# Chunk gating: two norms folded into column factors and one number per token, LayerNorm's affine in the mixing's eviction, mixing between the u units

## The chip, the cores and the metric

The kernel is one program on one core of a Trainium2 chip (trn2). The metric is device time of one execution in microseconds, as a median of runs. A profiled execution gives the trace; its own time stands beside its span below.

## The reference

Two transformer-like blocks work on 512 tokens of 1024 channels in float32. The change lies where the first block ends and the second begins.

```python
h = h + conv_ffn(hn, ...)                      # end of the first block ("ffout" in the kernel)
x = rms_norm(h, norm_final_g)                  # output of the first block, the second block's residual stream
y = _rms_norm(x, mix_norm_g[0])
# _chunk_gating_mixer(y, ...)
uv = gelu(y @ w_in, approximate=False)         # w_in: 1024 x 2048
u, v = split(uv, 2)
v = layer_norm(v, ln_g, ln_b)                  # over 1024 channels of a token
v = v.reshape(B, 4, 128, 8, 128)               # 4 chunks of 128 tokens, 8 groups of 128 channels
w = where(causal, w_s, 0)                      # 8 x 128 x 128
gate = einsum('gts,bnsgc->bntgc', w, v) + b_s  # mixes positions in a chunk
x = x + (u * gate) @ w_out
```

`rms_norm(x, g)` is `x * rsqrt(mean(x * x) + eps) * g` with the mean over a token's channels. 

## The kernel before

Channels lie on the 128 partitions in eight tiles (`h[:, m, :]` is 128 channels by 512 tokens), tokens on the free axis. Each fp32 product is made of three matmuls with operands split into a high part in fp32r and the rest (`mm3`, L425 to L429): high by high, low by high, high by low. Weights come as a stream of units of 512 KB (128 x 1024): SyncE's queue loads a unit into one of two `raw` buffers (L450), ScalarE copies it to the high part (`hi`, L896), VectorE subtracts for the low part (`lo`, L1160), and there are four slots. `hi(u)` and `lo(u)` prepare unit u + 3, and `hi` waits until the unit four before it has been multiplied. A unit is 24 matmuls of 512 columns.

Each engine has its program written out by hand; all order is by semaphores. TensorE accumulates a unit in one of two PSUM banks (0 and 1), and VectorE evicts it (`s_free`). `residual` (L1179 ff.) adds an evicted unit to `h`; ScalarE then makes `xhi` (L904) and a square (L908), VectorE `xlo` (L1166), GpSimd adds up squares in `ssum` (L1682). `norm` (L516) multiplies `ssum` with a matrix of ones, ScalarE takes the root (L912), VectorE the reciprocal (L1171) into `rbc`, which the evictions of the next stage multiply with (`rows`, L1198).

After the last feed-forward residual ("ffout") the order is this. `norm("ffout")`; VectorE scales `h` tile by tile with `rbc` and the final gain (L1429), and ScalarE, VectorE and GpSimd make `xhi`, `xlo` and the squares of the scaled tiles ("final1"). cgv: the v half of the projection with tokens on the output's partitions, two halves f of four units, in each 96 matmuls; within the first, after two units, `norm("final1")`; after it `rbc` is transposed (L699) and one column per token block copied to `rtok`, by which the gelu's eviction scales (L1042). cgu: eight u units, evicted to `uf` (L1198), gelu in place (L1049). Beside them v is prepared: statistics (L1454, L1456), `layer_norm` on VectorE (L1466), gain and shift along the channels on GpSimd (L1725, L1726), and the split of v (L1175, L1176). Then mixing: eight groups of 12 matmuls of 128 columns each. VectorE adds the position bias, multiplies with u and splits (L1483 ff.), and cgout, eight units of the output projection, follows.

## Time and profile before

| | us |
|---|---|
| median of 3 runs | 1997.72 (1996.34 to 1999.89) |
| profiled execution | 1995.45 |
| its span | 1993.7 |
| TensorE busy | 1929.3 (97%) |
| VectorE busy | 1148.2 (58%) |
| ScalarE busy | 657.5 (33%) |
| GpSimd busy | 175.9 (9%) |
| granted TensorE clock, mean | 0.983 |

Busy time is the sum of instruction durations. A matmul's end is modelled and matmuls overlap: one of 512 columns is shown with 0.39 us, while the next starts 0.23 us later. So durations of TensorE are read from start to start or from a stretch, and a row of a busy share near 100% says nothing of speed. [...]

### The profile page before, as it was taken

The numbers are of one execution on the slowest core, as the hardware profiler recorded it, in microseconds if no ns is written. First come the engines' busy times: TensorE is split into PE (matmuls) and PEld (weight loads), VectorE is DVE, ScalarE is ACT, GpSimd is POOL, SyncE is SP. The second block draws the span as 40 slices with busy tenths as digits, with TensorE's granted clock in tenths as the row PEclk, the third lists the DMA queues.
The fourth block names the chain that finished last, engine by engine and source line by source line (L and its number), as shares of the span: only waits on it lengthen the run. The fifth ranks groups of instructions, "written<-read, shape, count | busy, mean of one in ns | idle before, by whom it ended". The sixth has DMA issues, their size and how long they took to land.

```text
span 1993.7 us, 24668 instructions
## 1 busy us (share of the span) xinstructions
PE 1929.3 (97%) x9086; PEld 1587.7 (80%) x9086; DVE 1148.2 (58%) x1454; ACT 657.5 (33%) x871; POOL 175.9 (9%) x167
## 2 busy tenths in 40 slices
PE   6989999999999999799999999999999999999998
PEld 4878888778888887588888888888788777888886
DVE  5774767757766523777553245346666776424532
ACT  5214545343333322432322122323333343212221
POOL 2000221220000000240100000100000020000000
PEclk9989999999999999897999999999999999999998
DMA  4212222223323333221233353222222213232331
GB/s 139 75 58 70 75 68 70 85 83 108 95 95 95 105 106 106 97 84 63 93 100 96 97 135 98 93 96 79 74 69 80 64 48 116 95 98 93 97 103 64
DMA packets 55565, 177.64 MB, mean 89 GB/s; under 512 B 5891, under 2 KB 12179, under 8 KB 55356
## 3 DMA queue, kind: packets, MB, share of 16 engines
q1 hardware_dynamic: 46800, 168.32, 26.7%
q10 hardware_dynamic: 8684, 8.18, 1.5%
q8 instruction: 59, 0.97, 0.2%
q14 instruction: 22, 0.18, 0.0%
HBM read 173.26 MB, written 2.13 MB: 88 GB/s over the span
## 4 chain that ended last, share of the span: by engine, by line
PE 87%; DVE 8%; ACT 2%; issue 1%; DMA 1%; POOL 1%; ACTq 0%; DVEq 0%; SPq 0%; POOLq 0%
PE ps L427 27%; PE ps L428 27%; PE ps L429 27%; DVE wlo L1160 1%; PE ps L622 1%; PE ps L751 1%; PE ps L435 1%; PE ps L780 1%; PE ps L763 1%; DVE rbc L1171 1%; POOL ssum L1682 1%; PE ps L781 0%; PE ps L516 0%; DMA lgb<-lngb 0%; DVE vr L1176 0%
## 5 line engine op out<-in xcount | busy, mean ns | idle before, releaser
L427 PE MATMUL ps<-xhi,whi 128*128 128x512 f32 x1592 | 635.9, 399 | 20.5 <-DVE wlo L1160 12.9
L429 PE MATMUL ps<-xlo,whi 128*128 128x512 f32 x1592 | 623.1, 391 | 0.0
L428 PE MATMUL ps<-xhi,wlo 128*128 128x512 f32 x1592 | 622.8, 391 | 0.0
L1160 DVE TENSOR_TENSOR wlo<-raw,whi 128x1024 fp32r<-128x1024 f32 x317 | 408.8, 1290 | 259.4 <-ACT whi L896 258.6
L896 ACT ACTIVATE whi<-raw 128x1024 fp32r<-128x1024 f32 x317 | 333.0, 1053 | 526.7 <-PE ps L429 448.8
L427 PEld LDWEIGHTS ps<-xhi,whi 128*128 128x128 f32 x1592 | 300.7, 189 | 93.3 <-issue 16.5
L429 PEld LDWEIGHTS ps<-xlo,whi 128*128 128x128 f32 x1592 | 300.4, 189 | 64.0
L428 PEld LDWEIGHTS ps<-xhi,wlo 128*128 128x128 f32 x1592 | 300.9, 189 | 60.3 <-issue 1.4
L427 PE MATMUL ps<-mh,whi 128*128 128x512 f32 x512 | 199.3, 389 | 0.0
L428 PE MATMUL ps<-mh,wlo 128*128 128x512 f32 x512 | 199.2, 389 | 0.0
L429 PE MATMUL ps<-mh,whi 128*128 128x512 f32 x512 | 199.2, 389 | 0.0
L1059 ACT ACTIVATE ms<-mr 128x512 f32<-128x512 f32 x64 | 40.4, 632 | 229.0 <-DVE mr L1498 229.0
L427 PEld LDWEIGHTS ps<-mh,whi 128*128 128x128 f32 x512 | 96.1, 188 | 20.3 <-issue 0.4
L429 PEld LDWEIGHTS ps<-mh,whi 128*128 128x128 f32 x512 | 96.1, 188 | 20.1
L428 PEld LDWEIGHTS ps<-mh,wlo 128*128 128x128 f32 x512 | 96.1, 188 | 19.9
L1682 POOL TENSOR_TENSOR ssum<-ssum,sq 128x512 f32<-128x512 f32 x55 | 80.7, 1467 | 287.1 <-ACT sq L908 285.1
L1191 DVE TENSOR_TENSOR h<-h,ps 128x512 f32 x48 | 33.0, 688 | 105.6 <-PE ps L429 105.6
L1498 DVE SCALAR_TENSOR_TENSOR mr<-ps,rbc 128x512 f32<-128x512 f32 x64 | 44.2, 690 | 80.0 <-PE ps L429 80.0
L1679 POOL COPY ssum<-sq 128x512 f32<-128x512 f32 x8 | 5.7, 706 | 911.2 <-ACT sq L908 911.2
L904 ACT ACTIVATE xhi<-h,par 128x512 fp32r<-128x512 f32 (+1 forms) x48 | 34.6, 722 | 143.8 <-DVE h L1191 126.3
L427 PE MATMUL ps<-hid,whi 128*128 128x512 f32 x176 | 68.5, 389 | 0.0
L428 PE MATMUL ps<-hid,wlo 128*128 128x512 f32 x176 | 68.5, 389 | 0.0
(290 smaller groups left out, 2154.3 us busy)
## 6 DMA issues: line engine op xcount, KB each, us to landing
raw<-wst SPq DMA_DIRECT2D x317, 512.0 KB, 3.5
h<-xT ACTq DMA_DIRECT2D x8, 256.0 KB, 6.4
out<-h SPq DMA_DIRECT2D x8, 256.0 KB, 2.1
oP<-oB ACTq DMA_DIRECT2D x16, 66.0 KB, 2.2
lgb<-lngb ACTq DMA_DIRECT2D x1, 1024.0 KB, 7.3
bias_a<-bias_rows ACTq DMA_DIRECT2D x4, 256.0 KB, 9.4
...
```

What stands on the lines that cost most here:

```text
L427: pe.matmul(o, w[0], x[0], start=first, stop=False, **kw)
L428: pe.matmul(o, w[1], x[0], start=False, stop=False, **kw)
L429: return pe.matmul(o, w[0], x[1], start=False, stop=done, **kw)
L435: ins = pe.matmul(o, w[a], v[b], start=first and i == 0, stop=i == 2, skip_group_check=True)
L622: ins = pe.matmul(o, w, sspr[:, part, x, CO[d]:CO[d] + T - P * d], start=False, stop=True, skip_group_check=True)
L896: act.activation(whi[:, n % SLOTS, :], raw[:, n % 2, :], ACT.Copy).then_inc(s_hi, 1)
L904: act.activation(xhi[:, m, :], hm, ACT.Copy, scale=par[:, 8 * g + m:8 * g + m + 1] if mi is None else par[:, bass.ds(mi + 8 * g, 1)]).then ...
L1059: act.activation(ms[:, m % 2, :], mr[:, m % 2, :], ACT.Square).then_inc(s_ms, 1)
L1160: dve.tensor_tensor(wlo[:, n % SLOTS, :], raw[:, n % 2, :], whi[:, n % SLOTS, :].bitcast(F32), ALU.subtract).then_inc(s_split, 1)
L1191: dve.tensor_tensor(hm, hm, bank((a + m) % 2), ALU.add).then_inc(s_free, 1)
L1498: dve.scalar_tensor_tensor(mr[:, m % 2, :], acc, 0.0, rbc[:, :], ALU.max, ALU.mult).then_inc(s_free, 1)
L1682: ins = pool.tensor_tensor(ssum[:, :], ssum[:, :], sq[:, n % 2, :], ALU.add)
```

## The change

The two norms in front of the gating become column factors and one number per token. With h the residual and g the final gain, `rms_norm(rms_norm(h, g), g2)` is h times g times g2 (per channel, made once as `G_X1`) times one number per token, 1 / sqrt(mean((g*g + eps) * h * h) + eps * eps). So "ffout" makes `xhi`/`xlo` directly from `h` with the factor `G_X1`, and two squares per tile: of `h`, and of `h` times sqrt(g*g + eps) (`G_C1`). GpSimd sums both (`ssum`, `ssum2`); TensorE reduces them to one number per token (`token_sums`), and `spread` writes both numbers out over a bank each. `h` itself is scaled with the final norm during the second half of cgv (`first_block_normed`).

LayerNorm's gain and shift leave v. Both are per channel, which is the partition of the mixing's output: the gain multiplies there in the eviction, and the shift times the sum of a row of the mixing weights is added to the position bias (`wsf` times ones on TensorE, then eight operations on `bsb`). ScalarE makes v's high part. GpSimd's two operations per token block and the 1 MB load of `lgb` go.

The mixing groups stand behind u units 3 to 7 (`SPATIAL_BEHIND`), and the u units accumulate in banks 6 and 7. The first two output units take their first six k tiles each before the last two (`early=6`).

The diff is cut to its core; left out are semaphore names, buffers, constants and the loading of the two LayerNorm rows as columns of `par`.

```diff
+CGU_BANKS = (6, 7)
+SPATIAL_BEHIND = {3: (0,), 4: (1, 2), 5: (3, 4), 6: (5, 6), 7: (7,)}
...
+            def two_units(u, a, xs, early):
+
+                for ks in (range(early), range(early, UT)):
+                    for j in range(2):
+                        if ks[0] == 0:
+                            unit_ready(u + j)
+                            acc_wait(a + j)
+                        for k in ks:
+                            ins = mm3(pe, bank((a + j) % 2), w_tile((u + j) % SLOTS, k), xs(k), k == 0, k == UT - 1)
+                        if ks[-1] == UT - 1:
...
+            def token_sums():
+
+                pe.wait_ge(s_ss, S0["ffout"] + 2 * KD)
+                for n, src in enumerate((ssum2, ssum)):
+                    for t in range(NT):
+                        ins = pe.matmul(bank(7)[:, NT * n + t:NT * n + t + 1], src[:, t * P:(t + 1) * P], ones[:, 0:1],
+                                        start=n == 0 and t == 0, stop=True, skip_group_check=True)
+                ins.then_inc(s_cts, 1)
+
+            def spread():
+
+                pe.wait_ge(s_ctk, 1)
+                for n in range(2):
+                    for t in range(NT):
+                        ins = pe.matmul(bank(7 - n)[:, t * P:(t + 1) * P], rtk[:, NT * n + t:NT * n + t + 1].to_broadcast([P, P]), ident,
+                                        start=t == 0, stop=True, skip_group_check=True)
+                ins.then_inc(s_csp, 1)
+
+            def positions_mixed(g):
+
+                if g == 0:
+                    pe.wait_ge(s_r, R0["ug"])
+                    pe.wait_ge(s_wsr, 1)
+                    pe.wait_ge(s_bs2, 1)
+                if g >= 4:
+                    pe.wait_ge(s_sgv, g - 3)
+                for t in range(NT):
+                    ins = mm3(pe, bank(2 + g % 4)[:, t * P:(t + 1) * P], (vr[:, 0, t, g * P:(g + 1) * P], vr[:, 1, t, g * P:(g + 1) * P]),
+                              (wsr[:, 0, g, :], wsr[:, 1, g, :]), t == 0, True, skip_group_check=True)
...
-                        norm("final1")
+                        token_sums()
                     if f == 0 and j == 3:
-                        pe.wait_ge(s_rb, N0["final1"] + 1)
...
-            dense(U0["cgu"], A0["cgu"], full(8), x_tile)
-            pe.wait_ge(s_r, R0["ug"])
-            pe.wait_ge(s_cdv, 2)
...
+            pe.wait_ge(s_cpo, 1)
+            pe.wait_ge(s_cac, 4)
+            for n in range(2):
+                ins = pe.matmul(bank(4 + n), ones, wsf[:, 4 * n:4 * n + 4, :], start=True, stop=True)
+            ins.then_inc(s_wsm, 1)
+            pe.wait_ge(s_h2, KD)
+            for m in range(KD):
+                dense(U0["cgu"] + m, A0["cgu"] + m, full(1), x_tile, banks=CGU_BANKS)
+                for g in SPATIAL_BEHIND.get(m, ()):
+                    positions_mixed(g)
...
+            act.wait_ge(s_gns, 1)
+            act.activation(par[:, 8 * G_C1:8 * G_C1 + KD], par[:, 8 * G_C1:8 * G_C1 + KD], ACT.Sqrt, bias=eps[:, 0:1]).then_inc(s_gnc, 1)
...
-            residual("ffout", 2, 12, 4, None, "ffout")
+            act.wait_ge(s_gnc, 1)
+            with act.Fori(0, 2, 1) as i:
+                for m in range(4):
+                    for j in range(3 * m, 3 * m + 3):
+                        hi(U0["ffout"] + j, i, 12)
+                    act.wait_ge(s_free, at(A0["ffout"] + m + 1, i, 4))
+                    sn, k = S0["ffout"] + 2 * m, i * 4 + m
+                    act.wait_ge(s_ss, at(sn, i, 8))
+                    gain = lambda g: par[:, bass.ds(k + 8 * g, 1)]
+                    act.activation(xhi[:, k, :], h[:, k, :], ACT.Copy, scale=gain(G_X1)).then_inc(s_xhi, 1)
+                    act.activation(sq[:, 0, :], h[:, k, :], ACT.Square).then_inc(s_sqd, 1)
+                    act.activation(sq[:, 1, :], h[:, k, :], ACT.Square, scale=gain(G_C1)).then_inc(s_sqd, 1)
...
-            act.dma_start(lgb[:, :, :], lngb.partition_broadcast(P)).then_inc(s_cld, 16)
-            for m in range(KD):
-                act.wait_ge(s_rb, N0["ffout"] + 1)
-                act.wait_ge(s_cv, KF + m + 1)
-                x_hi(m, None, G_MIX2, S0["final1"] + m)
...
+            hi(U0["cgv"] + 1)
+            act.wait_ge(s_cts, 1)
+            for n, e in enumerate((eps2, eps)):
+                act.activation(rtk[:, NT * n:NT * n + NT], bank(7)[:, NT * n:NT * n + NT], ACT.Sqrt, bias=e[:, 0:1], scale=1.0 / D).then_inc(s_ctr, 1)
+            hi(U0["cgv"] + 2)
+            hi(U0["cgv"] + 3)
...
+            def v_hi(t):
+                act.wait_ge(s_lnd, t + 1)
+                act.activation(vr[:, 0, t, :], vt[:, t, :], ACT.Copy).then_inc(s_vhi, 1)
+
+            def u_gelu(m):
+                act.wait_ge(s_free, A0["cgu"] + m + 1)
+                act.activation(uf[:, m, :], uf[:, m, :], ACT.Gelu).then_inc(s_gu, 1)
+
+            hi(U0["cgu"])
+            act.wait_ge(s_agg, 1)
+            act.activation(mv[:, :, 2], mv[:, :, 1], ACT.Sqrt, bias=eps[:, 0:1]).then_inc(s_lns, 1)
+            v_hi(0)
+            v_hi(1)
+            hi(U0["cgu"] + 1)
+            v_hi(2)
+            v_hi(3)
+            for m in range(2, KD):
+                u_gelu(m - 2)
                 hi(U0["cgu"] + m)
-                act.wait_ge(s_free, A0["cgu"] + m + 1)
-                act.activation(uf[:, m, :], uf[:, m, :], ACT.Gelu).then_inc(s_cac, 1)
+            u_gelu(KD - 2)
+            u_gelu(KD - 1)
             residual("cgout", 2, 4, 4, G_MLP2, "cgout")
 
...
+            g_fin = par[:, 8 * G_FIN:8 * G_FIN + KD]
+            dve.tensor_tensor(par[:, 8 * G_X1:8 * G_X1 + KD], g_fin, par[:, 8 * G_MIX2:8 * G_MIX2 + KD], ALU.mult)
+            dve.tensor_tensor(par[:, 8 * G_C1:8 * G_C1 + KD], g_fin, g_fin, ALU.mult).then_inc(s_gns, 1)
...
-            residual("ffout", 2, 12, 4, None)
-            inverse_rms("ffout")
-            dve.wait_ge(s_sqd, S0["final1"])
-            for m in range(KD):
-                dve.scalar_tensor_tensor(h[:, m, :], h[:, m, :], par[:, 8 * G_FIN + m:8 * G_FIN + m + 1], rbc[:, :],
-                                         ALU.mult, ALU.mult).then_inc(s_cv, 1)
-                if m:
-                    dve.wait_ge(s_cv, KF + m)
-                    x_lo(m - 1, X0["final1"] + m - 1, G_MIX2)
-            dve.wait_ge(s_cv, KF + KD)
-            x_lo(KD - 1, X0["final1"] + KD - 1, G_MIX2)
...
+            dve.wait_ge(s_ctr, 2)
+            dve.reciprocal(rtk[:, :], rtk[:, :]).then_inc(s_ctk, 1)
+            lo(U0["cgv"] + 2)
+            lo(U0["cgv"] + 3)
+            dve.wait_ge(s_cpo, 1)
+            split(wsr[:, 0, :, :], wsr[:, 1, :, :], wsf[:, :, :], s_wsr)
...
+            chain(dve.tensor_copy(rbc[:, :], bank(7)))
+            for j in range(4):
+                lo(U0["cgv"] + 4 + j)
+                for m in (2 * j, 2 * j + 1):
+                    first_block_normed(m)
+                statistics(0, j)
             for t in range(NT):
...
+            lo(U0["cgu"])
+            dve.wait_ge(s_cld, 32)
+            dve.wait_ge(s_wsm, 1)
+            for g in range(KD):
+                ins = dve.scalar_tensor_tensor(bsb[:, g, :], bank(4 + g // 4)[:, g % 4 * P:(g % 4 + 1) * P], par[:, C_LNB + g:C_LNB + g + 1],
+                                               bsb[:, g, :], ALU.mult, ALU.add)
+            ins.then_inc(s_bs2, 1)
+            dve.wait_ge(s_lns, 1)
+            chain(dve.reciprocal(mv[:, :, 3], mv[:, :, 2]))
...
+            def v_lo(t):
+                dve.wait_ge(s_vhi, t + 1)
+                dve.tensor_tensor(vr[:, 1, t, :], vt[:, t, :], vr[:, 0, t, :].bitcast(F32), ALU.subtract).then_inc(s_r, 1)
...
-                dve.tensor_tensor(m4, b4, row, ALU.add).then_inc(s_cdv, 1)
-                dve.wait_ge(s_cdv, 4 + g)
+                dve.scalar_tensor_tensor(m4, b4, par[:, C_LNG + g:C_LNG + g + 1], row, ALU.mult, ALU.add).then_inc(s_sgv, 1)
...
+            layer_norm(0)
+            layer_norm(1)
+            u_rows(0)
+            lo(U0["cgu"] + 1)
+            v_lo(0)
+            layer_norm(2)
+            v_lo(1)
+            layer_norm(3)
+            u_rows(1)
+            lo(U0["cgu"] + 2)
+            v_lo(2)
+            v_lo(3)
+            for m in range(2, KD):
+                u_rows(m)
+                if m + 1 < KD:
+                    lo(U0["cgu"] + m + 1)
+                for g in SPATIAL_BEHIND.get(m, ()):
+                    gated(g)
             residual("cgout", 2, 4, 4, G_MLP2)
             inverse_rms("cgout")
 
...
-            sum_squares("ffout")
-            pool.wait_ge(s_cld, 48)
+            for m in range(KD):
+                for n, dst in ((2 * m, ssum), (2 * m + 1, ssum2)):
+                    pool.wait_ge(s_sqd, S0["ffout"] + n + 1)
+                    if m == 0:
+                        ins = pool.tensor_copy(dst[:, :], sq[:, n % 2, :])
+                    else:
+                        pool.wait_ge(s_ss, S0["ffout"] + n - 1)
+                        ins = pool.tensor_tensor(dst[:, :], dst[:, :], sq[:, n % 2, :], ALU.add)
...
-            sum_squares("final1")
-            pool.wait_ge(s_cld, 48)
-            for t in range(NT):
-                v = vt[:, t, :]
-                pool.wait_ge(s_lnd, t + 1)
-                chain(pool.tensor_tensor(v, v, lgb[:, 0, :], ALU.mult))
-                pool.tensor_tensor(v, v, lgb[:, 1, :], ALU.add).then_inc(s_lng, 1)
```

VectorE in front of cgv. Of the kernel before, from the last residual's addition on; `rbc` is the reciprocal root over all tokens:

```order
L1191 TENSOR_TENSOR h<-h,ps 128x512
...
L1171 RECIPROCAL rbc<-rtmp 128x512
L1429 SCALAR_TENSOR_TENSOR h<-h,par,rbc 128x512 x2
L1166 SCALAR_TENSOR_TENSOR xlo<-h,par,xhi 128x512
...
L1160 TENSOR_TENSOR wlo<-raw,whi 128x1024
L1171 RECIPROCAL rbc<-rtmp 128x512
L1160 TENSOR_TENSOR wlo<-raw,whi 128x1024 x3
L1443 COPY rtok<-ps 128x1 x4
```

Of the changed kernel, the same place; `rtk` holds the two numbers of each token:

```order
L1281 TENSOR_TENSOR h<-h,ps 128x512
...
L1256 SCALAR_TENSOR_TENSOR xlo<-h,par,xhi 128x512
...
L1250 TENSOR_TENSOR wlo<-raw,whi 128x1024 x2
L1523 RECIPROCAL rtk<-rtk 128x8
L1250 TENSOR_TENSOR wlo<-raw,whi 128x1024 x2
L1265 CAST wsr<-wsf 128x1024
L1266 TENSOR_TENSOR wsr<-wsf,wsr 128x1024
L1538 COPY rbc<-ps 128x512
L1250 TENSOR_TENSOR wlo<-raw,whi 128x1024
L1534 SCALAR_TENSOR_TENSOR h<-h,par,ps 128x512 x2
```

The two wide reciprocals and the scaling of `h` no longer stand between the last residual and x; the scaling has moved behind the weight splits of cgv's second half.

VectorE between the statistics and the last part of v, in the kernel before:

```order
L1456 BN_AGGR mv<-st 128x2 x4
L1160 TENSOR_TENSOR wlo<-raw,whi 128x1024
L1198 TENSOR_TENSOR uf<-ps,rbc 128x512
L1465 RECIPROCAL mv<-mv 128x1
L1466 TENSOR_SCALAR vt<-vt,mv 128x1024
...
L1175 CAST vr<-vt 128x1024
L1176 TENSOR_TENSOR vr<-vt,vr 128x1024
```

And in the changed one:

```order
L1547 BN_AGGR mv<-st 128x2 x4
L1250 TENSOR_TENSOR wlo<-raw,whi 128x1024
L1553 SCALAR_TENSOR_TENSOR bsb<-ps,par,bsb 128x128 x8
L1557 RECIPROCAL mv<-mv 128x4
L1561 TENSOR_SCALAR vt<-vt,mv 128x1024 x2
L1288 TENSOR_TENSOR uf<-ps,rbc 128x512
L1250 TENSOR_TENSOR wlo<-raw,whi 128x1024
L1565 TENSOR_TENSOR vr<-vt,vr 128x1024
L1561 TENSOR_SCALAR vt<-vt,mv 128x1024
```

Before, one normalisation stands behind each of the first four u evictions and one split behind each of the last four. Now all of it stands between u evictions 0 and 2, with two weight splits between.

TensorE around the u units, before and then now (a row of three for each `mm3`; "..." leaves out the repetitions):

```order
L429 MATMUL ps<-xlo,whi 128x512
L427 MATMUL ps<-wsr,vr 128x128
L428 MATMUL ps<-wsr,vr 128x128
L429 MATMUL ps<-wsr,vr 128x128
...
L427 MATMUL ps<-ugh,whi 128x512
```

```order
L768 MATMUL ps<-wsf,con 128x512 x2
L449 MATMUL ps<-xhi,whi 128x512
...
L449 MATMUL ps<-wsr,vr 128x128
L450 MATMUL ps<-wsr,vr 128x128
L451 MATMUL ps<-wsr,vr 128x128
...
L449 MATMUL ps<-ugh,whi 128x512
```

Before, 192 wide matmuls are followed by all 96 of the mixing. Now two sums over positions come first, then four units (96 wide ones), 12 of the mixing, a unit, 24, a unit, 24, a unit, 24, a unit and 12.

## Rows read from the trace of the kernel before

**Rows 1.** The page, busy us, share of the span, instructions.

```profile
PE 1929.3 (97%) x9086; PEld 1587.7 (80%) x9086; DVE 1148.2 (58%) x1454; ACT 657.5 (33%) x871; POOL 175.9 (9%) x167
```

**Rows 2.** Table by stretches: us, busy per engine (count), granted clock, DMA share, GB/s.

```profile
794.86:805.98 11.12, 1.29 (x4) 0.33 (x3) 6.35 (x6) 4.32 (x6) 1.26 (x1) 0.70 0.60 212
805.98:818.62 12.64, 12.64 (x48) 10.10 (x48) 10.19 (x11) 6.41 (x12) 8.46 (x7) 0.86 0.04 16
818.62:823.90 5.28, 1.11 (x4) 0.45 (x3) 5.28 (x4) 2.65 (x4) 3.85 (x3) 0.93 0.00 0
823.90:859.06 35.16, 34.89 (x149) 28.00 (x148) 17.39 (x19) 11.59 (x13) 0.00 (x0) 0.96 0.36 117
859.06:902.84 43.78, 43.78 (x194) 36.04 (x192) 39.51 (x37) 17.88 (x25) 23.85 (x8) 1.00 0.28 87
902.84:905.63 2.79, 0.15 (x1) 0.00 (x0) 2.71 (x4) 1.58 (x2) 0.00 (x0) 0.89 0.51 135
905.63:926.18 20.55, 20.55 (x97) 20.55 (x97) 16.97 (x28) 0.00 (x0) 0.00 (x0) 0.50 0.02 8
```

**Rows 3.** Timeline of TensorE: start, us, instruction, [idle before, releaser].

```profile
805.98 0.76 PE L427 MATMUL ps<-whi,xhi 128*128 128x512 f32 x1 [6.70 <-DVE xlo L1166]
...
822.94 1.94 PE L516 MATMUL ps<-ssum,con 128*128 128x512 f32 x2 [4.17 <-POOL ssum L1682]
```

**Rows 4.** Timelines of VectorE, GpSimd and ScalarE around the first norm and the first gelu.

```profile
792.07 1.23 DVE L1160 TENSOR_TENSOR wlo<-raw,whi 128x1024 fp32r<-128x1024 f32 x1 [4.21 <-ACT whi L896]
795.18 0.69 DVE L1191 TENSOR_TENSOR h<-h,ps 128x512 f32 x1 [1.88 <-PE ps L429]
...
796.84 1.26 POOL L1682 TENSOR_TENSOR ssum<-ssum,sq 128x512 f32<-128x512 f32 x1 [13.67 <-ACT sq L908]
...
836.73 1.28 ACT L1042 ACT_TABLE_LOAD   x1 [1.69 <-PE ps L429]
838.03 2.43 ACT L1042 ACTIVATE vt<-ps,rtok 128x512 f32<-128x512 f32 x4
```

**Rows 5.** Timeline of TensorE, fp32 matmuls (two records each).

```profile
1980.40 0.95 PE L874 MATMUL ps<-con,ssum 128*128 128x1 f32 x8
...
1983.62 2.07 PE L879 MATMUL ps<-con,rtok 128*128 128x128 f32 x8 [0.56 <-DVE rtok L1662]
...
99.31 1.88 PE L571 MATMUL ps<-gatt,con 128*128 128x512 f32 x4
```

**Rows 6.** Timeline of VectorE beside the u units; then two groups (busy, mean ns, idle).

```profile
863.15 0.94 DVE L1456 BATCH_NORM_AGGREGATE mv<-st 128x2 f32<-128x12 f32 x4
...
867.89 0.81 DVE L1466 TENSOR_SCALAR vt<-vt,mv 128x1024 f32<-128x1024 f32 x1
...
873.03 2.11 DVE L1466 TENSOR_SCALAR vt<-vt,mv 128x1024 f32<-128x1024 f32 x1
...
891.43 3.30 DVE L1176 TENSOR_TENSOR vr<-vt,vr 128x1024 fp32r<-128x1024 f32 x1
...
904.36 1.22 DVE L1176 TENSOR_TENSOR vr<-vt,vr 128x1024 fp32r<-128x1024 f32 x1
...
L1608 DVE TENSOR_TENSOR oB<-ps,oB 128x128 f32<-128x128 f32 x16 | 4.6, 290 | 14.4 <-ACT oB L1109 14.4
L896 ACT ACTIVATE whi<-raw 128x1024 fp32r<-128x1024 f32 x317 | 333.0, 1053 | 526.7 <-PE ps L429 448.8
```

**Rows 7.** Timeline of TensorE, short matmuls behind wide ones; then two stretches.

```profile
86.94 0.22 PE L427 MATMUL ps<-gatr,gtok 128*128 128x128 f32 x1
...
89.66 2.53 PE L435 MATMUL ps<-gqk,gstr 64*128 64x64 f32 x42
...
926.18:928.85 2.67, 2.67 (x8) 2.09 (x9) 2.57 (x5) 0.00 (x0) 0.00 (x0) 0.50 0.00 0
1368.00:1380.00 12.00, 12.00 (x80) 9.64 (x79) 8.38 (x15) 5.17 (x12) 0.00 (x0) 1.00 0.14 45
```

More of the change, by code:

```diff
@@ L183, in end, with build @@
         self.i = None
-def build(nc, wst, xT, prm, cst, wup, wsT, bs, lngb, rb, onehot, fdram, out):
+def build(nc, wst, xT, prm, cst, wup, wsT, bs, rb, onehot, fdram, out):
     es = ExitStack()
@@ L264, in build @@
             mv = sb("mv", [P, NT, 4], F32, m)
-            rtm = lgb[:, :, 0:T]
         with ExitStack() as m:
@@ L497, in fresh, with loop @@
                 return tile
-            def loop(name, turns, nu, groups, xs, made, count, before=None, done=0):
+            def two_units(u, a, xs, early):
[7 more added lines that the diff above has]
+                        if ks[-1] == UT - 1:
+                            ins.then_inc(s_unit, 1)
+            def loop(name, turns, nu, groups, xs, made, count, before=None, done=0, early=0):
                 u, a, g = U0[name], A0[name], len(groups)
@@ L504, in loop @@
                     dense(u, a + done, groups[done:], xs, free=True)
+                elif early:
+                    two_units(u, a, fresh(xs, made, count), early)
+                    dense(u, a + 2, groups[2:], xs)
                 else:
@@ new lines, in _ @@
+            hi(U0["cgv"] + 1)
[4 more added lines that the diff above has]
+            hi(U0["cgv"] + 3)
+            act.wait_ge(s_ctk, 1)
+            for f in range(2):
+                if f:
+                    for j in range(4, 8):
+                        hi(U0["cgv"] + j)
@@ L1040, in _ @@
                 act.wait_ge(s_unit, U0["cgv"] + 4 * f + 4)
                 for t in range(NT):
-                    act.activation(vt[:, t, f * T:(f + 1) * T], bank(CG_BANKS[f][t]), ACT.Gelu, scale=rtok[:, t:t + 1]).then_inc(s_cac, 1)
-            act.wait_ge(s_cdv, 3)
-            for t in range(NT):
-                act.activation(mv[:, t, 2:3], mv[:, t, 1:2], ACT.Sqrt, bias=eps[:, 0:1]).then_inc(s_cac, 1)
-            for m in range(KD):
+                    act.activation(vt[:, t, f * T:(f + 1) * T], bank(CG_BANKS[f][t]), ACT.Gelu, scale=rtk[:, t:t + 1]).then_inc(s_cac, 1)
@@ L1434, in _ @@
-            dve.wait_ge(s_cv, KF + KD)
-            x_lo(KD - 1, X0["final1"] + KD - 1, G_MIX2)
-            lo(U0["cgv"])
-            inverse_rms("final1")
-            for j in range(1, 4):
-                lo(U0["cgv"] + j)
-            dve.wait_ge(s_cpe, 1)
-            for t in range(NT):
-                ins = dve.tensor_copy(rtok[:, t:t + 1], bank(7)[:, t * P:t * P + 1])
-            ins.then_inc(s_cdv, 1)
-            dve.wait_ge(s_cpo, 1)
-            split(wsr[:, 0, :, :], wsr[:, 1, :, :], wsf[:, :, :], s_cdv)
@@ L1447, in _ @@
-            dve.wait_ge(s_cld, 48)
-            for f in range(2):
-                if f:
-                    for j in range(4, 8):
-                        lo(U0["cgv"] + j)
-                for t in range(NT):
-                    dve.wait_ge(s_cac, NT * f + t + 1)
-                    chain(dve.bn_stats(st6[:, t, f, :], vt[:, t, f * T:(f + 1) * T]))
+            dve.wait_ge(s_gnc, 1)
+            residual("ffout", 2, 12, 4, G_X1)
+            lo(U0["cgv"])
+            lo(U0["cgv"] + 1)
+            dve.wait_ge(s_ctr, 2)
@@ L1464, in layer_norm @@
                 v = vt[:, t, :]
-                chain(dve.reciprocal(mv[:, t, 3:4], mv[:, t, 2:3]))
                 dve.tensor_scalar(v, v, mv[:, t, 0:1], mv[:, t, 3:4], ALU.subtract, ALU.mult).then_inc(s_lnd, 1)
-            for m in range(KD):
-                lo(U0["cgu"] + m)
-                rows(U0["cgu"] + m, A0["cgu"] + m, uf[:, m, :])
-                if m < NT:
-                    layer_norm(m)
-                if m >= NT:
-                    t = m - NT
-                    dve.wait_ge(s_lng, t + 1)
-                    split(vr[:, 0, t, :], vr[:, 1, t, :], vt[:, t, :], s_r)
@@ L1477, in _, with u_rows, gated @@
-            for g in range(KD):
-                dve.wait_ge(s_cpe, 2 + g)
-                dve.wait_ge(s_cac, 12 + g + 1)
+            def v_lo(t):
+                dve.wait_ge(s_vhi, t + 1)
+                dve.tensor_tensor(vr[:, 1, t, :], vt[:, t, :], vr[:, 0, t, :].bitcast(F32), ALU.subtract).then_inc(s_r, 1)
+            def u_rows(m):
+                a = A0["cgu"] + m
+                rows(U0["cgu"] + m, a, uf[:, m, :], b=CGU_BANKS[a % 2])
+            def gated(g):
+                dve.wait_ge(s_spa, g + 1)
+                dve.wait_ge(s_bs2, 1)
```

106 lines of the change are left out of this document (60 added, 46 removed).

## The prediction

> **What bounds the kernel now.** I read the page's busy table first. TensorE is busy 97% of the span, the next engine 58% [rows 1]: a change pays only what it takes from TensorE's own line, in work, in waiting or in clock. So the second view is the table by stretches, cut where TensorE changes its work [rows 2]. The changed part runs from the last feed-forward matmul (issued until 794.86 us) to the first matmul of the gating output (926.18): 131.32 us. The v units (cgv, 192 matmuls of 512 columns) should need what the 192 of the u units need, 43.8 us in the fifth stretch, 0.228 each; they are spread over the second and fourth.
>
> The rest of the front, 859.06 - 794.86 - 43.8 = 20.4 us, is this. The first stretch, 11.12 us, is the wait for the last sum of squares, a reduction, and 6.70 us for the normed x [rows 3]. The second holds 48 matmuls in 12.64 us where 10.9 would do: after the pause the clock is low, 1.7 us lost. The third, 5.28 us, is the second norm, 4.17 of it a wait for GpSimd's sum [rows 3]. The fourth holds 144 in 35.16 where 32.8 would do: a slow start again, four transposes, and a short wait for the first gelu, 2.3 us. [...]
>
> **The front.** The x operand of cgv now comes out of the last residual as h times a column factor, and the first eviction multiplies by one number per token. At 794.86 its tiles 0 to 6 are made. Tile 7 needs the add, 0.69 us [rows 4], a ScalarE copy and a VectorE difference of the same 512 columns, which I take alike; with hand-overs it is there by 799, and cgv reads it 7 x 2.74 = 19 us after its start. Units cgv0 to cgv2 are already split, the last by the row at 792.07 [rows 4]. So no wait there: 11.12 and 5.28 us of pauses and the two low-clock starts go. The eight tiles of h itself are scaled later, on VectorE beside cgv's second half: 0.7 us each, 5.6 in 21.9 us.
>
> Added on TensorE's line are token_sums, eight fp32 matmuls into one column, and spread, eight of 128 columns. The end of this kernel has both forms: four of the first take 0.95 us (eight records), so eight take 2.0; four of the second take 2.07 us [rows 5], with the low clock behind a pause, and at full clock I take half, 2.1 for eight, bounds 1.6 and 4.1. Their inputs are early: GpSimd now sums 16 squares instead of eight, 1.26 us each [rows 4], two per tile against a tile every 15 us; the last is done near 801, and token_sums stands at 805.8. The roots, a table load of 1.28 us [rows 4] and the reciprocal lie beside the 11 us of cgv2 and cgv3. The first gelu comes a table load and 0.6 us [rows 4] after the half; spread and the first two token tiles, 1.4 us, cover it. New front: 43.8 + 2.0 + 2.1 = 47.9 us against 64.2: **16.3 us less**.
>
> **The back.** Call T the end of cgv. VectorE sets when mixing may begin, so I walk its new order with the durations of [rows 6]. Aggregates are there at T + 5.0 (864.09 against 859.06). Then a weight split 1.2; eight position-bias operations of 128x128 out of PSUM, which the trace lacks: the nearest, with two inputs of that size, is 0.29 each, 2.3 us together, bounds 1 and 3; reciprocal and two normalisations at 0.81: T + 10.3; a u eviction 0.7. ScalarE now makes v's high half, at 1.05 each like its weight copies, and stands between: v0, v1, then the weight copy are done at T + 12.6, so the split ends at 13.8, v-lo 0 at 15.0, and normalise, v-lo 1, normalise, u eviction at 18.5. TensorE meanwhile: position sums, two fp32 matmuls of 512, 1.9 us [rows 5], u0 to T + 7.4, u1 to 12.8, u2 to 18.3; u3 finds its bank at 18.5. ScalarE then has v2, v3, a table load, a gelu and a weight copy, to T + 21.9; the split and the last two v-lo make T + 25.6. TensorE is there at T + 24.0, and waits 1.6 us. So the position sums cost nothing: they lie beside a chain that ends later.
>
> From there come four u units (21.9 us) and the mixing in bursts of 12, 24, 24, 24 and 12. Its price at full clock is in the trace: 24 matmuls of the same form take 2.72 us (86.94 to 89.66 [rows 7]), 0.113 each, against 0.214 in the old block. 96 x 0.113 = 10.9. VectorE has four operations per gated group, about 2.6 us, and 1.9 us per unit, at most 7.1 us against TensorE's 8.2; gated(7) hides behind 36 early matmuls of the output units. New back: 25.6 + 21.9 + 10.9 = 58.4 against 67.1: **8.7 us less**. Behind the old block the first six wide matmuls take 2.67 us at clock 0.50 instead of 1.4 [rows 7]; with a full-clock unit ahead, **1.3 us** go too.
>
> The gains come to 26.3 us. Against them I set one fall of the clock in the new order, 1.6 us (as the two of the front): behind token_sums, behind spread, or at the 1.6 us wait with a burst behind it. Three VectorE operations of 128x8 and one root, ahead of the feed-forward, stand beside a streaming TensorE and cost nothing; without that cover under 1 us. **Net 24.7 us.** The profiled execution took 1995.45 us for a span of 1993.7; the median of the runs is 1997.72, 2.27 above. 1995.45 - 24.7 = 1970.8, at the level of the median 1973.0.
>
> [...] In the third stretch the mean clock of 0.93 puts the fall 4.5 us into the pause, in the sixth 0.89 puts it 2.2 us in [rows 2]: the same kind of pause, no fixed moment. [...]
> The first normalisation took 0.81 us, the next 2.11, while GpSimd's gain and shift ran beside it, and a v-lo 3.30 with and 1.22 without them [rows 6]. [...]
>
> **Rivals.**
> A, the clock stays low through the bursts. For it: the old mixing ran all its 20.55 us at 0.50. Against: that block came behind a pause and had nothing wide between. Price: 0.214 instead of 0.113, 96 times, is 9.7 us, and 1.5 us behind two of the bursts 3 more: 1973 + 13 = **1986**; half of it, **1980**.
> B, v's preparation stays slow and mixing starts late: the change does not do there what it says. If the long durations hold (2.11 for 0.81 four times, 3.30 for 1.22 in four v-lo and two weight splits [rows 6]), that is 5.2 + 12.5 = 17.7 us on the chain that ends at T + 25.6, all of it TensorE's wait: **1991**. Against: no GpSimd work is left in that stretch.
> C, slower. One mechanism: from token_sums on, the clock stays at its lower level, because a short or one-column piece comes back every 5 to 10 us. Wide matmuls then take the 0.44 of the slow start (2.67 us for six [rows 7]) instead of 0.228. Each us of low clock loses 0.5, so it decides from 53 of the 106 us on. If all of it were low: 288 wide ones by 0.21, 61 us, and the mixing's 9.7, less 24.7, is 46 us slower: **2044**. Against: from 1368 to 1380 us, with short matmuls between wide ones, the clock is 1.00 [rows 7].
>
> **Chances.** Forecast (full clock but for a fall or two, v ready near T + 26) 0.72, own range 1966 to 1978. A 0.13, B 0.10, C 0.02, and 0.03 for something unseen that eats most or all of the gain. A measurement of this kernel can tell 0.2%, 4 us, from no change. Faster 0.95, same 0.02, slower 0.03. The range for 8 in 10: below, no fall, no wait, and a run as fast as the fastest shown, 1966; above, half of A and the upper bound of spread, 1982.
>
> **What would show it.** Right: cgv begins within 0.3 us of the last feed-forward matmul; no pause over 1 us before the u units; T 48 us behind that matmul; the first mixing matmul 25.6 us behind T; mixing matmuls 0.11 apart at a granted clock near 1.00; 106 us in all. Wrong: mixing 0.21 apart (A); the first burst later than T + 30 (B); a clock of 0.5 over whole units (C); or a pause in cgv for a weight split or for the token numbers, which I have at nothing.

## The result and the profile after

| | before | after |
|---|---|---|
| median of 6 runs each | 1996.01 (1993.39 to 1999.89) | 1985.53 (1982.68 to 1988.2) |
| profiled execution | 1995.45 | 1985.68 |
| its span | 1993.7 | 1983.9 |
| TensorE busy | 1929.3 | 1934.9 |
| GpSimd busy | 175.9 | 151.3 |

The ratio is 0.9941, with a 95% interval of 0.993 to 0.9951: about 11 us faster, where 24.7 were forecast. 1985.5 lies outside the range of 1966 to 1982.

The page's busy row, as [rows 1] of before. TensorE has 28 instructions more and 5.6 us more busy time:

```profile
PE 1934.9 (98%) x9114; PEld 1576.8 (79%) x9114; DVE 1127.3 (57%) x1453; ACT 660.0 (33%) x873; POOL 151.3 (8%) x160
```

The table by stretches of the changed kernel, cut as [rows 2] (stretch, its length, busy us and count for TensorE, its weight loads, VectorE, ScalarE, GpSimd, then the granted clock as a share of full speed, DMA share and GB/s):

```profile
801.46:812.40 10.94, 10.94 (x49) 9.03 (x49) 5.49 (x4) 5.16 (x6) 3.82 (x3) 1.00 0.62 205
812.44:814.14 1.70, 1.70 (x18) 1.70 (x16) 0.00 (x0) 0.00 (x0) 0.00 (x0) 1.00 0.43 171
...
825.15:826.85 1.70, 1.70 (x17) 1.70 (x16) 0.00 (x0) 1.45 (x2) 0.00 (x0) 1.00 0.07 27
826.85:848.73 21.88, 21.88 (x100) 18.11 (x98) 13.27 (x17) 6.39 (x8) 0.00 (x0) 1.00 0.30 94
848.73:850.04 1.31, 1.31 (x5) 0.59 (x4) 0.32 (x1) 1.11 (x2) 0.00 (x0) 1.00 0.11 44
850.04:872.68 22.64, 22.35 (x98) 18.00 (x96) 17.35 (x31) 13.26 (x16) 0.00 (x0) 1.00 0.20 61
872.68:904.47 31.79, 31.79 (x185) 28.02 (x186) 26.88 (x39) 7.02 (x9) 0.00 (x0) 1.00 0.27 90
```

TensorE's timeline at the joints of these stretches (start, us, engine, instruction, in brackets the idle time before it and what ended it), which answers to [rows 3]:

```profile
801.30 0.39 PE L451 MATMUL ps<-hid,whi 128*128 128x512 f32 x1
801.53 0.39 PE L449 MATMUL ps<-whi,xhi 128*128 128x512 f32 x1
...
812.44 1.84 PE L717 MATMUL ps<-con,ssum 128*128 128x1 f32 x16
...
825.15 1.95 PE L726 MATMUL ps<-con,rtk 128*128 128x128 f32 x16
...
848.73 1.88 PE L768 MATMUL ps<-wsf,con 128*128 128x512 f32 x4
...
872.68 0.33 PE L449 MATMUL ps<-wsr,vr 128*128 128x128 f32 x1 [0.29 <-DVE vr L1565]
872.85 0.28 PE L450 MATMUL ps<-wsr,vr 128*128 128x128 f32 x1
...
905.14 0.27 PE L451 MATMUL ps<-wsr,vr 128*128 128x128 f32 x1
905.26 0.45 PE L449 MATMUL ps<-ugh,whi 128*128 128x512 f32 x1
```

The reader is to see that in the changed part nothing is lost any more. cgv starts 0.23 us behind the last feed-forward matmul, no pause is over 0.3 us, and the granted clock is 1.00 in every stretch. From 801.53 to the first output matmul at 905.26 are 103.7 us, where before had 131.3 [rows 2]: 27.6 less, more than forecast. But the whole is only 9.8 us shorter (1995.45 to 1985.68). The last feed-forward matmul is issued at 801.30 in place of 794.63, 6.7 us later; and from the norm behind cgout (956.02, before 976.51) to the end are 1027.9 us, where before has 1017.2: 10.7 us more, in stages that the diff does not touch.

These stages are seen best in a stretch without joints: 384 matmuls in a row that multiply by `mh` (there are four such stretches), from the first one's start to the last one's. First of the kernel before, then of the changed one, both at the full clock and with the same work on every engine:

```profile
1236.29:1323.11 86.82, 86.82 (x385) 71.91 (x384) 33.91 (x33) 25.44 (x31) 9.60 (x7) 1.00 0.31 102
```

```profile
1217.86:1307.23 89.37, 89.37 (x385) 71.62 (x383) 33.89 (x33) 25.40 (x31) 9.58 (x7) 1.00 0.31 100
```

From one start to the next that is 86.82 / 383, 226.7 ns, before and 89.37 / 383, 233.3 ns, after. The 528 matmuls with `hid`, the first block's last, in the same two kernels, at clock 1.00 in both:

```profile
675.18:794.63 119.45, 119.45 (x528) 98.91 (x527) 38.10 (x35) 29.14 (x31) 8.37 (x7) 1.00 0.34 106
```

```profile
678.33:801.30 122.97, 122.97 (x529) 98.55 (x528) 48.26 (x42) 37.65 (x45) 17.69 (x14) 1.00 0.32 104
```

119.45 / 527 is 226.7 ns, 122.97 / 527 is 233.3. Matmuls with `xhi` and `xlo` stand as close as before. The 384 in a row ahead of the `mh` stretch above start from 1149.25 to 1236.07 us before and from 1130.80 to 1217.63 after: 86.82 and 86.83 us, 226.7 ns each, at clock 1.00. Over the whole timeline, leaving out distances over 0.3 us, the mean from start to start is 227.4 ns before and 227.6 after (4709 and 4699 distances).

What differs is where the moving operand lies. The changed kernel's small tiles are larger (34 more numbers of 4 bytes in `par`, one in `eps2`, eight in `rtk`, 192 bytes in all as the built kernels place them: 128 for `par`, 32 each for the other two), and what is allocated behind them starts 192 bytes later in the partition: `hid` and `mh` at byte 120,896 for 120,704, `yr` at 174,144 for 173,952. `ugh` and `ugl` start 3,904 bytes earlier, because `rtm` is half as large as `lgb`, which stood in its place; modulo 256 that is the same shift by 192. The weight slots (24,704) and `xhi` (73,856) lie ahead of the small tiles and stay.

### The profile page after: what moved, and what is told of

Read it like the earlier page. It is cut to its first block, busy times and chain, and to the rows that moved or that the text cites. A ratio compares the mean times of both kernels' runs of the same rounds, so it can differ in the third digit from the quotient of the medians.

```text
span 1983.9 us, 24733 instructions
## 1 busy us (share of the span) xinstructions
PE 1934.9 (98%) x9114; PEld 1576.8 (79%) x9114; DVE 1127.3 (57%) x1453; ACT 660.0 (33%) x873; POOL 151.3 (8%) x160
## 4 chain that ended last, share of the span: by engine, by line
PE 88%; DVE 8%; ACT 2%; issue 1%; POOL 1%; DMA 0%; ACTq 0%; DVEq 0%; SPq 0%; POOLq 0%
PE ps L449 28%; PE ps L451 27%; PE ps L450 27%; DVE wlo L1250 1%; PE ps L659 1%; PE ps L815 1%; PE ps L457 1%; PE ps L844 1%; PE ps L827 1%; DVE rbc L1261 1%; POOL ssum L1796 1%; PE ps L845 0%; DVE yr L1265 0%; DVE gatt L1305 0%; PE ps L858 0%
## 5 line engine op out<-in xcount | busy, mean ns | idle before, releaser
L449 PE MATMUL ps<-mh,whi 128*128 128x512 f32 x512 | 202.0, 395 | 0.0
L451 PE MATMUL ps<-mh,whi 128*128 128x512 f32 x512 | 201.9, 394 | 0.0
L1796 POOL TENSOR_TENSOR ssum<-ssum,sq 128x512 f32<-128x512 f32 x41 | 61.1, 1491 | 190.1 <-ACT sq L972 188.7
L449 PE MATMUL ps<-hid,whi 128*128 128x512 f32 x176 | 69.3, 394 | 0.0
L451 PE MATMUL ps<-hid,whi 128*128 128x512 f32 x176 | 69.3, 394 | 0.0
L1256 DVE SCALAR_TENSOR_TENSOR xlo<-h,par,xhi (+1 forms) x48 | 42.7, 892 | 42.9 <-ACT xhi L968 33.3
```

The lines of the kernel that those rows point to most:

```text
L449: pe.matmul(o, w[0], x[0], start=first, stop=False, **kw)
L451: return pe.matmul(o, w[0], x[1], start=False, stop=done, **kw)
L1256: dve.scalar_tensor_tensor(xlo[:, m, :], h[:, m, :], gain, xhi[:, m, :].bitcast(F32), ALU.mult, ALU.subtract).then_inc(s_x, 1)
L1796: ins = pool.tensor_tensor(ssum[:, :], ssum[:, :], sq[:, n % 2, :], ALU.add)
```

## Experiments

The kernel before was run beside each on the same chip. Where traces are compared below, "the changed part" is the time from the last feed-forward matmul's start to that of cgout's last: 176.2 us in the kernel before, 148.6 in the changed one, 147.5 in one and in seven.

### One: the changed kernel with 64 bytes put in

```diff
         rtok = sb("rtok", [P, NT])
+        pad = sb("pad", [P, 16])
```

> The changed kernel with a tile of 64 bytes per partition added behind the small tiles, so that every tile allocated after it (hid, mh, yr, ugh and others) starts 64 bytes later. Theory (placement): in the changed kernel these tiles start at 64 modulo 128 bytes, before at 0, and a 512-column matmul whose moving operand lies there comes every 233.3 ns instead of 226.7; with the tile they are back at 0, all such matmuls at 226.7, and some 2700 of them give back about 17 us: 1968 us, against about 1996 for the kernel before. Rival (work of GpSimd, or data and power, slows the feed-forward): the spacing stays 233.3 and the time about 1985.

Measured: 1969.19 (1965.69 to 1970.41) against 1997.37, ratio 0.9855 (0.9838 to 0.9871). The same stretch of `mh`:

```profile
1208.22:1295.03 86.81, 86.81 (x384) 71.91 (x383) 33.91 (x33) 25.43 (x31) 9.60 (x7) 1.00 0.31 102
```

The old spacing is back, and the time is 28.2 us below the kernel before, where the prediction's sum had 24.7. A tile that nobody reads is worth 0.86% of the kernel, some 17 us. By count: `hid` 528, `mh` 1536, `yr` and `ug` 192 each, about 2450 matmuls times 6.6 ns are 16.2 us.

### Two to four: the kernel before, shifted by 64, 128 and 32 bytes

The same line in the kernel before, with 16, 32 or 8 numbers.

> The kernel before, with the same tile of 64 bytes and nothing else. Theory (placement): matmuls that read hid, mh, yr, ugh as moving operand go from 226.7 to 233.3 ns, those of xhi (which lies ahead of the tile) stay at 226.7; 17 us slower, about 2013. Rival: no change, 1996.

> The kernel before with a tile of 128 bytes. If a multiple of 128 bytes is what counts: spacing 226.7 everywhere and 1996 us. If 256 or more counts (the start goes from 128 to 0 modulo 256), or if any shift counts: another spacing for hid and mh.

> The kernel before with a tile of 32 bytes: the tiles behind it start at 32 modulo 128. If only a multiple of 128 is good: 233.3 ns for hid and mh, about 2013 us. If the loss grows with something finer (32-byte pieces against 64-byte ones): more than 233.3. If only 64 is bad: 226.7.

Measured: 64 bytes 2005.52 (2004.44 to 2007.69), ratio 1.0044 (1.0027 to 1.0061) against 1997.37; 128 bytes 2013.1, 32 bytes 2015.99, one run each. So no other part of the change is needed to slow the kernel. Of the expectations, 233.3 ns and 17 us for 64 bytes failed (228.9 ns and 8 us), and so did the rule behind them, that a start at a multiple of 128 bytes is good: 128 bytes cost as much as 32. The `mh` stretch of the first two:

```profile
1241.62:1329.30 87.68, 87.68 (x385) 71.93 (x384) 33.91 (x33) 25.44 (x31) 9.63 (x7) 1.00 0.33 101
```

```profile
1246.68:1336.04 89.36, 89.36 (x384) 71.88 (x383) 33.94 (x33) 25.44 (x31) 9.63 (x7) 1.00 0.32 99
```

With 32 bytes it is 89.37 us too (1248.29 to 1337.66). It is not a slope: 32, 128 and 192 bytes cost the whole 2.55 us, 64 bytes a third of it, 256 nothing.

### Five and six: is it the address, or the distance from the weights?

In five, 128 bytes stand ahead of the weight slots, so that weights and moving operands shift together. In six, 128 bytes ahead and 128 behind the weight slots, so that the weights shift by 128 and all else by 256.

```diff
         raw = sb("raw", [P, 2, UT * P])
+        pad = sb("pad", [P, 32])
         whi = sb("whi", [P, SLOTS, UT * P], F32R)
         wlo = sb("wlo", [P, SLOTS, UT * P], F32R)
+        pad2 = sb("pad2", [P, 32])          # in six only
```

> The kernel before with 128 bytes put ahead of the weight slots, so that all operands (weights, xhi, hid, mh) start 128 bytes later and keep their distances. What is known: shifts of hid and mh alone by 32, 64, 128 and 192 bytes gave 233.3, 228.9, 233.3 and 233.3 ns, 256 gave 226.7. Theory R (relative): the place of the moving operand against that of the weights counts, modulo 256; all spacings stay 226.7 ns and the time 1997. Theory A (absolute): the place itself modulo 256 counts; all wide matmuls, those of xhi too, take 233.3 ns; some 7700 of them, 50 us slower, about 2047.

> The kernel before with 128 bytes ahead of the weight slots and 128 behind them: the weights move by 128 bytes, all else by 256. Theory R: the distances change by 128, as in the run with 128 bytes behind the small tiles, but for xhi too: 233.3 ns for every wide matmul, about 2047 us. Theory A, if the moving operand's own place counts: 226.7 ns and 1997 us. Theory A, if the weights' own place counts: 233.3 ns.

Measured, one run each: 2000.36 and 2035.21 against 1994.55. The `mh` stretch of five, then of six:

```profile
1241.42:1328.24 86.82, 86.82 (x385) 71.90 (x383) 33.89 (x33) 25.44 (x31) 9.60 (x7) 1.00 0.32 101
```

```profile
1262.63:1352.00 89.37, 89.37 (x385) 71.92 (x383) 33.91 (x33) 25.44 (x31) 9.62 (x7) 1.00 0.32 100
```

Five moved every operand by the 128 bytes that cost 2.54 us in three, and keeps 86.82. Six moves `mh` by a harmless 256 and only the weights by 128, and has 89.37. There the matmuls with x stand wider as well, 232.7 ns by the same mean over the timeline, for 227.4 in the kernel before: the 384 in a row ahead of `mh` take 89.37 us (1173.03 to 1262.40) for 86.82. That is why it loses 41 us (I had expected 233.3 and 50). So in these runs it is the distance between the moving operand and the weights that counts, and a shift of 256 bytes changes nothing (86.81 us in one). In the kernel before, `hid` and `mh` start 96,000 bytes behind the weights, 375 times 256. Five's own time is 5.8 us above the kernel before, in a single run, with all spacings the old ones. In its trace the extra time lies ahead of `hid`, which begins at 680.36 where it begins at 675.18 in the trace of the kernel before, and its mean granted clock is 0.979 against 0.984 in the run beside it; seven, below, begins `hid` as late with the program of one. So it is a difference between executions and not the placement.

### Seven and eight: mixing in one block again

Seven is the kernel of one once more, the partner for the next three on their chip. Eight puts all 96 mixing matmuls behind the last u unit.

```diff
-SPATIAL_BEHIND = {3: (0,), 4: (1, 2), 5: (3, 4), 6: (5, 6), 7: (7,)}
+SPATIAL_BEHIND = {7: (0, 1, 2, 3, 4, 5, 6, 7)}
```

> The changed kernel with 64 bytes more, again, as the measure for the three runs beside it: 1969 us.

> As the run beside it, with all eight mixing groups behind the last u unit instead of behind units 3 to 7. Theory (the mixing was slow before because it ran as one block at low clock): v is ready long before, no wait; 96 matmuls in one stretch behind a wide unit at 0.11 us for the first 5 us or so, then the clock falls and the rest takes 0.21, and the first wide ones behind it are slow: 5 to 8 us more; besides VectorE's gating, 2.6 us a group, then runs without cover and TensorE waits for it: 20.5 us for eight groups against 10.9 to 20 of mixing, partly hidden by the 36 early matmuls. In all 7 to 12 us slower than the run beside it. Rival (bursts have no worth of their own): within 2 us of it.

Measured: seven 1972.04 (1968.71 to 1973.42), eight 1972.97 (1972.56 to 1975.17), against 1998.88; ratios 0.9858 (0.9841 to 0.9874) and 0.9871 (0.9855 to 0.9888). My theory of 7 to 12 us failed and the rival held. The block in eight in two stretches, then the two waits that end in it and behind it:

```profile
889.14:899.16 10.02, 9.49 (x85) 9.35 (x84) 8.88 (x15) 1.58 (x2) 0.00 (x0) 1.00 0.02 5
899.16:900.55 1.39, 1.39 (x12) 1.39 (x13) 1.32 (x3) 0.00 (x0) 0.00 (x0) 1.00 0.00 0
```

```profile
899.16 0.33 PE L450 MATMUL ps<-wsr,vr 128*128 128x128 f32 x1 [0.53 <-DVE rtm L1578]
...
906.23 0.50 PE L450 MATMUL ps<-ugh,whi 128*128 128x512 f32 x1 [1.62 <-DVE ugl L1267]
```

84 short matmuls stand in a row (889.14 to 898.35), 0.111 us apart, and the clock stays at 1.00. The old block took 20.55 us at 0.50 [rows 2]. So spreading the mixing did not buy the fast clock. It bought waits: in the traces the changed part takes 151.0 us in eight and 147.5 in seven, since TensorE waits 0.97 us for an eviction and the 0.53 and 1.62 us above for gated tiles, in seven only 0.28. The medians are too coarse for these 3.5 us: the four runs of seven alone span 4.7, and its profiled execution is slower than eight's by 4.5 us ahead of cgv, where the two kernels are the same.

### Eleven: the same block behind a pause

Of the kernel before, one thing is left that could have lowered the clock: the 2.79 us without a matmul ahead of the block. Eleven makes such a pause in kernel eight.

```diff
             for m in range(2, KD):
                 u_rows(m)
+                if m == KD - 1:
+                    dve.reciprocal(idle[:, :], rbc[:, :]).then_inc(s_late, 1)
...
                 if g == 0:
+                    pe.wait_ge(s_late, 1)
```

> The kernel with the 64 bytes and all 96 mixing matmuls in one block behind the u units, and in addition one VectorE reciprocal of 128 x 512 that writes a tile nobody reads; the first mixing matmul waits for it. What is computed stays whole. So TensorE stands still for about 4 us right ahead of the block. Theory (the block of mixing ran at the low clock in the kernel before because TensorE had stood still 2.79 us ahead of it, not because it is a block of short matmuls): the pause costs 3.5 to 4.5, the granted clock falls behind it, the 96 mixing matmuls run at about 0.21 in place of 0.11 (9.6 more), and some 1 us is lost in the slow start of cgout: 14 to 16 above the same kernel without the pause (its span 1970.9), so a span of about 1985 to 1987. Rival (a pause of this length costs only itself): 4 above, a span of about 1975, and mixing at 0.11.

Measured: 1988.43 in one run, span 1986.7, which is 15.8 above eight's 1970.9. TensorE's timeline, and the stretches of the pause, of the mixing and behind it:

```profile
891.27 0.39 PE L454 MATMUL ps<-xlo,whi 128*128 128x512 f32 x1
895.79 0.45 PE L452 MATMUL ps<-wsr,vr 128*128 128x128 f32 x1 [4.14 <-DVE idle L1602]
```

```profile
891.60:895.79 4.19, 0.06 (x1) 0.03 (x1) 3.95 (x2) 1.57 (x2) 0.00 (x0) 0.82 0.01 5
895.79:916.30 20.51, 20.51 (x96) 20.51 (x97) 16.95 (x28) 0.00 (x0) 0.00 (x0) 0.50 0.00 1
916.30:921.50 5.20, 5.20 (x13) 4.07 (x14) 4.05 (x6) 0.00 (x0) 0.00 (x0) 0.50 0.00 0
921.50:925.00 3.50, 3.50 (x16) 2.86 (x15) 0.00 (x0) 0.00 (x0) 0.00 (x0) 0.98 0.47 150
```

The block is back at 20.51 us. Behind it, 12 wide matmuls pass before the clock is up (the row's 13 count a short one that is still running). Of the 15.8 us, 2.3 lie ahead of cgv, where the two kernels are the same, so that the sum fell into the expected 14 to 16 is in part luck. The changed part is 13.6 longer than in eight: 4.3 from the pause and 9.1 in the block (20.51 for 11.41, of which eight waits 0.53). In the matmuls alone the block costs 9.8 more: 96 at eight's 0.111 would be 10.7. The slow start of cgout costs 2.5, about what eight loses there by its wait. So the one block is nearly as good as the bursts as long as no pause stands ahead of it, and what pays most is that v is ready in time.

### Nine: the token numbers ahead of cgv

`token_sums` and `spread` stand ahead of the first cgv unit, and ScalarE's root and VectorE's reciprocal ahead of the weight work for cgv.

```diff
+            token_sums()
+            spread()
             for f in range(2):
...
-                    if f == 0 and j == 1:
-                        token_sums()
-                    if f == 0 and j == 3:
-                        spread()
```

> As the run beside it, with token_sums and spread ahead of cgv, so that TensorE waits for the norm again, while the column factors stay. Theory (the front's gain is the hidden wait): TensorE waits for GpSimd's last two sums, the root, the reciprocal, about 6 to 8 us, and starts at low clock, 1.7: 8 to 10 us slower. Rival (the front's gain comes from leaving out the second norm alone): within 3 us.

Measured: 1980.89 (1979.61 to 1983.6), ratio 0.9911 (0.9894 to 0.9927): 8.9 above seven, as expected. Its stretches of the wait and of the two small steps:

```profile
796.95:802.53 5.58, 0.39 (x3) 0.00 (x1) 1.44 (x2) 3.14 (x4) 2.66 (x2) 0.93 0.73 264
802.53:810.28 7.75, 7.00 (x32) 6.92 (x33) 1.43 (x2) 1.36 (x3) 1.09 (x1) 0.50 0.09 19
```

The wait for GpSimd's last sum is 5.2 us, and behind it the clock is at 0.50: the two steps take 3.57 and 3.43 us, with a wait of 0.75 for the reciprocal between, 7.75 in all. The same instructions behind 48 wide matmuls each took 1.70 us, at clock 1.00. The changed part is 11.4 us longer than in seven's trace.

### Ten: GpSimd works beside v's preparation

Two products of 128 x 1024 on GpSimd per token block, on a tile that nobody reads, where the old gain and shift stood.

```diff
+            for t in range(NT):
+                pool.wait_ge(s_lnd, t + 1)
...
+                for _ in range(2):
+                    chain(pool.tensor_tensor(idle[:, :], idle[:, :], wsf[:, :, :]..., ALU.mult))
```

> As the run beside it, with GpSimd working as before while v is prepared: two 128x1024 products per token block on a tile of its own that nobody waits for. Theory (the two engines exclude each other): normalisations go from 0.8 to 2 us, v's low parts and weight splits from 1.2 to over 3, and mixing starts 8 to 15 us later, all of it TensorE's wait: 8 to 15 us slower. Rival (only GpSimd's place in the chain cost time, not its work): within 1 us.

Measured: 1981.79 (1979.89 to 1984.52), ratio 0.9913 (0.9897 to 0.993): 9.8 above seven. VectorE and GpSimd in ten, then the same operations in the changed kernel without GpSimd's work, to compare with [rows 6]:

```profile
859.37 2.87 DVE L1563 TENSOR_SCALAR vt<-vt,mv 128x1024 f32<-128x1024 f32 x1
862.15 3.36 DVE L1567 TENSOR_TENSOR vr<-vt,vr 128x1024 fp32r<-128x1024 f32 x1
...
868.18 0.68 DVE L1290 TENSOR_TENSOR uf<-ps,rbc 128x512 f32<-128x512 f32 x1
...
852.30 23.99 POOL L1850 TENSOR_TENSOR idle<-idle,wsf 128x1024 f32<-128x1024 f32 x8
```

```profile
862.45 0.81 DVE L1561 TENSOR_SCALAR vt<-vt,mv 128x1024 f32<-128x1024 f32 x1
863.17 1.22 DVE L1565 TENSOR_TENSOR vr<-vt,vr 128x1024 fp32r<-128x1024 f32 x1
```

and TensorE of ten:

```profile
869.01 0.76 PE L451 MATMUL ps<-xhi,whi 128*128 128x512 f32 x1 [7.99 <-DVE uf L1290]
...
878.56 0.33 PE L451 MATMUL ps<-wsr,vr 128*128 128x128 f32 x1 [2.47 <-DVE vr L1567]
```

The normalisation and v's low part take 2.87 and 3.36 us beside GpSimd's work, 0.81 and 1.22 without. The eviction out of PSUM keeps its 0.68. TensorE waits 7.99 us for a bank whose eviction stands behind these on VectorE, then 2.47 for v's last low part. Behind both the clock is low: its mean is 0.51 from 869.01 to 872.00 and 0.53 from 878.56 to 882.00. In the traces mixing begins 35.8 us behind the end of cgv, for 24.0 in seven, and the changed part is 15.0 us longer; ahead of and behind it ten's profiled execution is faster than seven's, so the medians show less. Ten is not the whole of rival B: GpSimd's work ends at 876.3, and only two normalisations (2.87, 2.82) and two low parts (3.42, 3.36) take the long durations, where B had four, four and two weight splits. So its price of 17.7 us stays untested.

### Twelve: without the order of the first two output units

```diff
-            loop("cgout", 2, 4, full(4), lambda k: (ugh[:, k, :], ugl[:, k, :]), s_r, R0["ug"], early=6)
+            loop("cgout", 2, 4, full(4), lambda k: (ugh[:, k, :], ugl[:, k, :]), s_r, R0["ug"])
```

> The kernel with the 64 bytes, without the option of cgout's loop that takes k = 7 out of the first output unit and puts it later (early=6), so that all units have the same order. What is computed stays whole. Theory (the last gated tiles are late for the first unit, as the prediction had it): TensorE waits 2 to 4 us at k = 7 of the first unit of cgout, and the time is 2 to 5 above the kernel with the option. Rival (the gated tiles are there in time because mixing is spread over the u units): no wait over 0.5 and the same time within 0.1%.

Measured: 1969.2 (1965.49 to 1973.07) against 1997.62, ratio 0.9866 (0.9848 to 0.9883): no loss. In its trace the last low part of the gated tile is written before it is wanted:

```profile
898.36 0.45 PE L450 MATMUL ps<-ugh,whi 128*128 128x512 f32 x1
```

```profile
900.53 0.69 DVE L1267 TENSOR_TENSOR ugl<-rtm,ugh 128x512 fp32r<-128x512 f32 x1
```

k = 7 of the first unit begins 21 matmuls behind 898.36, at 903.1, and the tile is there at 901.2. No pause over 0.3 us is in its trace from there through cgout, and the changed part takes 147.5 us, as in one. With only 12 mixing matmuls left at the end, plain order does. The best kernel found is thus the changed one with the 64 bytes, with or without this option.

## Why the prediction was wrong, point by point

The direction and the mechanism in the changed part were right, the size of the whole was not: 9.8 us less in the profiled execution for 24.7. **The step that failed is the sum's base: "1995.45 - 24.7 = 1970.8".** It takes every stage outside the changed part at its old time. In place of nothing, the stages that multiply by `hid`, `mh`, `yr` and `ug` lost about 16 us, 3.5 of them in `hid` (122.97 for 119.45 us) and 10.1 in four stretches of `mh` (2.5 each), because of 192 bytes of small tiles; for `yr` and `ug` 1.3 each by count. The small columns were counted as VectorE operations only ("cost nothing"), never as bytes. 0.03 was left for "something unseen that eats most or all of the gain", and it ate 60% of it. Experiment one takes the one cause out and gives 1969.19 and, again, 1972.04 in seven, against the forecast of 1973.0. Against the kernel before on their own chips that is 28.2 and 26.8 us less (28.4 in twelve) for 24.7. So the sum for the changed part was some 2 to 4 us short as well, for the reasons that the steps show: 1.6 for a fall of the clock that did not come, 1.6 for mixing that begins earlier, 0.7 in the front.

The steps, with the forecast first:

- **Gap in front of cgv**: none; 0.23 us from start to start, one matmul. Right.
- **`token_sums`, `spread`**: 2.0 and 2.1; 1.70 each at full clock. At the low clock, in nine, `spread` takes 3.43, below its upper bound of 4.1.
- **Front**: 47.9; 47.2 (801.53 to 848.73), 192 matmuls in 43.8 of it. Right, and the first gelu and the weight splits cost nothing, as said.
- **Position sums**: 1.9 us, hidden; 1.31 us of TensorE's line, hidden, since v ends later. The eight bias operations: 2.3 for the eight, 2.15 in the trace. Right.
- **Mixing starts at T + 25.6**: at T + 24.0 (872.68 against 848.73), with a wait of 0.29 us for 1.6. VectorE's starts are closer than its durations (a normalisation of 0.81 us is followed after 0.72, a low part of 1.22 after 1.14), and the aggregates end at T + 4.3 for 5.0. I had added durations up. Early by 1.6.
- **Four u units and 96 mixing matmuls**: 32.8; 32.6 (872.68 to 905.26). Right to 0.2.
- **One fall of the clock, 1.6**: none fell; 1.00 in all stretches above. None of the three places that I had named for it has a pause over 0.3 us. In the other runs the low clock comes behind pauses: 0.50 behind 4.14 us in eleven and 5.2 in nine, 0.51 and 0.53 behind 8.0 and 2.5 in ten. It does not come behind 84 short matmuls in a row, nor behind a wait of 1.6 us, in eight: 1.00. One reading of mine was wrong: I put a fall "4.5 us into the pause", but the wait in that stretch is 4.17 us [rows 3], so the fall is 4.5 us into the stretch, behind the end of the wait.
- **Slow start behind mixing, 1.3**: gone (0.28 us from the first output matmul to the second), but cgout's 192 matmuls pay 1.3 for their operand's place, so cgout is as long as before.

Front and back together: 25.0 less forecast, 27.6 measured. The old back in that sum, 67.1 us, is 859.06 to 926.18 in [rows 2], 20.55 of it mixing at 0.50. Rival A (mixing at 0.21) did not come, though its price for the mixing, 9.7, was right: eleven shows 9.8. What brings the low clock there is the pause ahead of the block (4.14 us, then 0.50) and not the short matmuls (1.00 in eight). Rival B did not come; ten shows what makes these operations long: 2.8 to 3.4 us each beside GpSimd products of 3.0 us, 0.81 and 1.22 without them. The eviction, which has one operand in PSUM, takes 0.68 in both. That the two engines exclude each other, the theory written down for ten, was my reading; the runs show the durations and not how they come about. Rival C did not come.

What is left of the 6.7 us ahead of cgv, after 3.5 for `hid` and 1.3 for `yr`, is under 2 us. Kernel one and seven, which are the same, have `hid` begin at 675.86 and 680.25, so this is within what one kernel shows from execution to execution. Behind cgout, 10.1 of the 10.7 us are the four `mh` stretches.
